# A weight piece of block 2's in-projection becomes filling work in the mixer attention

## The chip, the cores and the metric

One core of one Trainium2 chip. The metric is the device time of one execution in microseconds; 2487.95 us is the median of three runs of the kernel before.

## The reference, cut to what matters

Two transformer blocks of two layers each, at a model width of 1024 and 256 tokens; the change acts on block 2. Each of its layers computes, in the mixer:

```
z = h @ w_in                       # h: normed x, 256 x 1024
m_qk, m_v, m_o, m_i, m_f, c_glu, f_q, f_k, f_v, f_f = split(z)
hm = mlstm(silu(conv(m_qk)), m_v, m_i, m_f)   # 4 heads of 64, normed, times sigmoid(m_o)
hc = silu(layernorm(conv(a * sigmoid(g))))    # a, g = halves of c_glu
hf = softmax(f_q f_k^T / 8 + decay, causal) f_v    # 8 heads of 64
x = x + concat(hm, hc, hf) @ w_out
```

After it come attention over a memory of 256 rows (whose values are `mem_n @ w_kv`) and a feed-forward part. Everything is float32.

## The kernel before, in words

**Products.** All weights come as a stream of pieces of 1 MB, 128 x 2048, through a ring of 6 slots that SyncE fills. ScalarE rounds a piece to fp32r (`ring_hi`, line 235), VectorE takes the rest (`ring_lo`, line 238), and TensorE multiplies three times (high by high, high by low, low by high), all at line 244. A piece serves two groups of products (`pe_products`, line 264); a group is 8 tiles of the contraction by 3 matmuls, 24 matmuls of 256 columns into one bank of PSUM. `take_products` (line 307) is the other side, on ScalarE and VectorE: at the first group of a piece it first splits pieces ahead (`split_ahead`, line 224: two further pieces; at places one more), then waits for the group, copies its bank out, and runs its step for this group. TensorE runs its own step ahead of a group.

**The in-projection of block 2** has 26 groups (`b2_groups`, line 1781), 13 pieces. Groups 22 to 25 are the values of the eight softmax heads, one piece for heads 0 to 3 and one for 4 to 7, written to `tok`. Beside the groups runs the work on what they gave (lines 1812, 1847, 1905), at group numbers written out by hand: at CONV a convolution; at MEANS (17) TensorE's mean for the layer norm; in their step of group 18 VectorE centres (line 1955) and ScalarE loads a table and squares (line 1861, semaphore `head_squared`); at VARS (20) TensorE's matmuls for the variance, which wait for the two squares; in the step VARS ScalarE's root, in the step VARS + 1 VectorE's scaling (line 1967, semaphore `ln_scaled`), in the step VARS + 2 VectorE's split of one piece more; in ScalarE's step UNITS − 1 (22) a table load, six SiLUs (lines 1869, 1872) and the split of one piece more; in its step UNITS + 1 (24) another table load.

**The mixer attention** (`pe_attention`, line 705, and its two partners) goes over 12 pairs of heads and query tiles: 8 of softmax attention, 4 of the mLSTM. It has 15 steps. In step i TensorE makes the scores of pair i, turns (transposes, line 737) the probabilities of pair i − 2 and mixes pair i − 3 with the values. VectorE adds mask and takes the maximum into a score buffer (line 826), and scales by the inverse sum (line 852) one step later; ScalarE takes the exponentials (line 790), copies the turned probabilities (line 798) and the mixed output (line 803). Score buffers are three, of two halves, in `hT`, which lies over the low part of `h`. Output banks are 4 and 5 in turn for the first six pairs, then 4 alone. After TensorE's first scores all three engines meet (line 199): each waits until the others are through with the in-projection.

**Filling.** In steps 9 to 13 TensorE also works off the two groups of one later piece, the memory's values (`pe_value_fill`, line 2113), in bank 5: 16 steps of three matmuls, four amid steps 9, 10 and 11, two after 12 and 13. ScalarE copies them out in its steps 10 and 14 (line 321). In its step 0 ScalarE splits a piece ahead and, in steps 0 and 1, rounds two tiles of the convolution's output (line 516) for the out-projection, in the place where the high part of `h` was; VectorE takes their rests in steps 2 and 3 (line 521). The out-projection goes over its 8 tiles in the order MIXER_TILES, that in which they are split.

Of the kernel before, what the change touches and what calls it, by code (L numbers as in the profile page):

```python
# [107 lines left out]
def build(nc, A, y_out):  # L108
    with ExitStack() as ctx:
# [55 lines left out]
        def sem(name):  # L165
            if name not in sems:
                sems[name] = ctx.enter_context(nc.semaphore(name))
            return sems[name]
# [6 lines left out]
        def base(e, name):  # L175
            return seen.get((e.engine, name), 0)
# [505 lines left out]

        def s_buf(pair, i, e):
            b = 2 * (i % BUF) + e
            if "late" in pair:
                return Zt[:, 8 + b, 0:T]
            return hflat[:, b * 514:(b + 1) * 514] if pair["sinks"] else hT[:, b, 0:T]
# [1076 lines left out]
        def rms2(c):  # L1764
            return Zt[:, 12 + c, T:2 * T]

        MIXER_TILES = (2, 3, 4, 5, 6, 7, 0, 1)
        MIXER_BANKS = (0, 1, 6, 7)


# [10 lines left out]
        def b2_groups(layer):  # L1781
            g = feature_major([z2(8), z2(9)], 0, T)
            g += feature_major([z2(6), z2(7)], 0, T)
            for c in range(2):
                terms, rows_, n, _, held = g[c]
                g[c] = (terms, rows_, n, [("function", z2(8 + c), ACT.Sigmoid)], held)
                terms, rows_, n, _, held = g[2 + c]
                g[2 + c] = (terms, rows_, n, [("gated", CP[:, c, 30:30 + T], z2(8 + c), act_outs[layer] + c + 1)], held)
            g += feature_major([UP[:, 0, 3:259], UP[:, 1, 3:259]], 0, T)
            g += feature_major([UP[:, 2, 3:259], UP[:, 3, 3:259]], 0, T)  # L1790
            g += token_major([SG[:, t, :] for t in range(2)], n=16)
            g += token_major([tok[:, t * 768:t * 768 + 256] for t in range(2)])
            for out, (terms, rows_, n, _, held) in zip((z2(4), z2(5)), feature_major([None, None], 0, T)):
                g.append((terms, rows_, n, [("function", out, ACT.Sigmoid)], held))
            for j in range(2):
                g += feature_major([z2(10 + 2 * j), z2(11 + 2 * j)], 0, T, HD ** -0.5)
            for j in range(2):
                g += feature_major([z2(14 + 2 * j), z2(15 + 2 * j)], 0, T)
            for j in range(2):
                g += token_major([tok[:, t * 768 + 256 + 256 * j:t * 768 + 512 + 256 * j] for t in range(2)])  # L1800
            return g


        B2_WHO = ["act", "act", "dve", "dve"] + 22 * ["act"]
        act_outs = [0, 0]
        B2_BANKS = (2, 3, 0, 1)
        x_outs = [0, 0]

        gated_outs, heads_before = [0, 0], [0, 0]
        GATES, CONV, SUMS, MEANS, VARS, UNITS = 11, 14, 15, 17, 20, 23  # L1810

        def pe_mixer(pe, layer):

# [160 lines left out]
        def causal(q):  # L1974
            return const("masks", 512, 640) if q == 0 else const("masks", 384, 640)

        def fox_pairs():
            pairs = []
            for c in range(4):
                for q in range(TT):  # L1980
                    nk, at = (q + 1) * P, slice(q * P, (q + 1) * P)
                    pairs.append(dict(apart=None, turns=0, alone=c == 3, nk=nk, mask=causal(q), init=[3 * NEG] * 2, sinks=None,
                        scores=[[(Zt[r, 10 + c, at], Zt[r, 14 + c, 0:nk], nk), (row_of(4 + 2 * c + e), falls[:, 0:nk], nk)]
                                for e, r in enumerate(HALVES)],
                        v=[[fv(t, 2 * c + e) for t in range(q + 1)] for e in range(2)],
                        place=[(r, slice(0, P)) for r in HALVES], out=mixT[:, 4 + c, at]))
            return pairs

        def mlstm_pairs():
            pairs = []  # L1990
            for c in range(2):
                for q in range(TT):
                    nk, at = (q + 1) * P, slice(q * P, (q + 1) * P)
                    pairs.append(dict(turns=None, alone=True, nk=nk, mask=causal(q), init=[0.0] * 2, floor=[FC[:, q, 2 * c + e:2 * c + e + 1] for e in range(2)],
                        sinks=None, apart=[(Zt[r, c, at], Zt[r, 2 + c, 0:nk]) for r in HALVES],
                        scores=[[(row_of(2 * c + e), falls[:, 0:nk], nk)] for e in range(2)],
                        v=[[mv(t, 2 * c + e) for t in range(q + 1)] for e in range(2)],
                        place=[(r, slice(0, P)) for r in HALVES], out=Zt[:, 6 + c, at]))
            return pairs


        def act_mix_step(act, layer):

            def step(i):
                act_value_fill(act, i)
                if i < 2:
                    act.wait_ge(sem("conv_ready"), 2 * layer + i + 1)
                    act_split_mix(act, (2 + i,), T)
                c = (i - 5) // 2
                if i % 2 == 1 and 0 <= c < 4:  # L2010
                    act.wait_ge(sem("heads_out"), heads_before[layer] + 2 * c + 2)
                    act_split_mix(act, (4 + c,), T)
                if i == 13:
                    act_m_square(act, layer, 0)
            return step

        def dve_mix_step(dve, layer):

            def step(i):
                if i == 0:  # L2020
                    phase_others(dve)
                if i in (2, 3):
                    dve_split_mix(dve, (i,), T)
                c = (i - 7) // 2
                if i % 2 == 1 and 0 <= c < 4:
                    dve_split_mix(dve, (4 + c,), T)
                dve_value_fill(dve, i)
            return step
# [79 lines left out]


        FILL_BANK = 5  # L2110
        FILL_AMID, FILL_AFTER, FILL_OUT, FILL_PIECE = {9: 4, 10: 4, 11: 4}, {12: 2, 13: 2}, (10, 14), 12

        def pe_value_fill(pe, layer):
            groups, weights = value_groups(1), []
            todo = [(g, k) for g in range(2) for k in range(KT)]
            out = base(pe, "product_out_act")
            meet = meet_first(pe)

            def fill(n):
                for g, k in [todo.pop(0) for _ in range(n)]:  # L2120
                    if (g, k) == (0, 0):
                        pe.wait_ge(sem("heads_out"), heads_before[layer] + 6)
                        weights.extend(piece_slot(pe))
                    if (g, k) == (1, 0):
                        pe.wait_ge(sem("product_out_act"), out + 1)
                    stationary, moving = groups[g][0][k]
                    for m, (w, part) in enumerate(((weights[0], 0), (weights[0], 1), (weights[1], 0))):
                        last = k == KT - 1 and m == 2
                        mm(pe, bank[FILL_BANK][:, 0:T], stationary(w, part), moving(w, part), start=k == 0 and m == 0,
                           stop=last, last_of="product_in_act" if last else None)  # L2130
                    if (g, k) == (1, KT - 1):
                        stream["release"] = True
                        advance(pe, "product_out_act", 2)

            def amid(i):
                fill(FILL_AMID.get(i, 0))

            def between(i):
                meet(i)
                fill(FILL_AFTER.get(i, 0))  # L2140
            return dict(amid=amid, between=between)

        def act_value_fill(act, i):
            if i == 0:
                split_ahead(act, "act", 1)
                wanted["act"] -= 1
            if i == FILL_OUT[0]:
                take_products(act, "act", value_groups(1)[0:1], "act", at=(FILL_BANK,))
            if i == FILL_OUT[1]:
                take_products(act, "act", value_groups(1)[1:2], "act", at=(FILL_BANK,))  # L2150

        def dve_value_fill(dve, i):
            if i == FILL_PIECE:
                take_products(dve, "dve", value_groups(1), "act", at=(FILL_BANK,))

        def x_pairs(layer):
            return [dict(apart=None, turns=1, alone=False, nk=T, mask=const("masks", 128, 384), init=[3 * NEG] * 2, sinks=None,
# [613 lines left out]
        def _(pe):  # L2771
# [25 lines left out]
            for layer in range(DEPTH):  # L2797
# [5 lines left out]
                                inside=lambda k: pe_mean(pe, 4, (3, 4, 5, 6, 7), 0, T) if k == 3 else None)  # L2803
                pe_products(pe, b2_groups(layer), "h_split", B2_WHO, at=B2_BANKS, before=pe_mixer(pe, layer))
                pe.wait_ge(sem("product_out_act"), base(pe, "product_out_act") - 2)
                heads_before[layer] = base(pe, "heads_out")
                pe_attention(pe, fox_pairs() + mlstm_pairs(), **pe_value_fill(pe, layer))
                pe.wait_ge(sem("neg_max"), base(pe, "neg_max"))
# [407 lines left out]
```

## Time and profile before

| | |
|---|---|
| Median of three runs | 2487.95 us (2487.22 to 2489.45) |
| The profiled execution's own time | 2489.04 us |
| Its span, first to last instruction | 2487.3 us |
| Mean granted TensorE clock | 0.992 |
| TensorE matmuls busy | 2398.9 us (96%) |
| TensorE weight loads busy | 2042.9 us (82%) |
| VectorE busy | 1827.4 us (73%) |
| ScalarE busy | 1494.0 us (60%) |

Rows of the profile name a line of the kernel, an engine, an operation and its tiles, out<-in. PE is the TensorE matmul, PEld its weight load, DVE VectorE, ACT ScalarE. A clock of 1.00 is 2.4 GHz, 0.50 is 1.2 GHz. In a row of the timeline, brackets at the end give the engine's idle time before it and what ended it; a matmul's duration contains a tail in which the next one already runs.

### The profile page before, as it was taken

What the parts mean: (1) busy time and instruction counts of PE and PEld (TensorE: products, weight loads), DVE (VectorE), ACT (ScalarE), POOL (GpSimd) and SP (SyncE); (2) the same over time, 40 slices, a digit from 0 to 9 for tenths busy, and PEclk for the clock granted to TensorE, in tenths of its full rate; (3) what the DMA queues carried; (4) which work ended last, traced back from release to release, by engine and by line L of the source; (5) the groups of instructions that cost most, each with busy time, mean ns of one, the idle gap of its engine ahead of it and who ended that gap; (6) DMA issues with size and microseconds to landing.
All of it is one profiled execution on the core that took longest, in us unless ns stands there. A gap on an engine that the chain in (4) does not pass through costs nothing.

```text
span 2487.3 us, 38102 instructions
## 1 busy us (share of the span) xinstructions
PE 2398.9 (96%) x14832; PEld 2042.9 (82%) x14832; DVE 1827.4 (73%) x2487; ACT 1494.0 (60%) x1960; POOL 27.5 (1%) x86
## 2 busy tenths in 40 slices
PE   8997999999999899999999999989999999999998
PEld 6875788888887688898888889788888888888886
DVE  5548766566566777676666657578898898898997
ACT  4246465465444666556665545666777777777775
POOL 0000000000000000010000001000000000000000
PEclk9999999999999999999899999999999999999999
DMA  8245445555544555554235545146998998998996
GB/s 335 105 145 193 156 168 187 186 186 187 186 159 146 221 185 188 186 179 153 86 140 197 189 169 196 69 153 236 372 355 340 371 359 346 361 363 350 359 361 256
DMA packets 81640, 564.57 MB, mean 227 GB/s; under 512 B 9328, under 2 KB 12672, under 8 KB 13632
## 3 DMA queue, kind: packets, MB, share of 16 engines
q1 hardware_dynamic: 80144, 559.97, 60.3%
q0 software_dynamic: 1328, 2.25, 0.3%
q8 instruction: 119, 1.95, 0.3%
q14 instruction: 49, 0.40, 0.1%
HBM read 559.97 MB, written 1.05 MB: 226 GB/s over the span
## 4 chain that ended last, share of the span: by engine, by line
PE 60%; DVE 4%; ACT 3%; issue 1%; DVEq 0%; ACTq 0%
PE psum L244 58%; DVE ring_lo L238 1%; ACT ring_hi L235 1%; PE psum L2428 1%; PE psum L737 1%; ACT Z L798 0%; ACT hT L790 0%; DVE xT L337 0%; DVE hT L398 0%; DVE hT L1489 0%; ACT Z L790 0%; DVE xT L671 0%; DVE Z L1466 0%; DVE Z L1467 0%; DVE xT L669 0%
## 5 line engine op out<-in xcount | busy, mean ns | idle before, releaser
L238 DVE TENSOR_TENSOR ring_lo<-ring,ring_hi 128x2048 fp32r<-128x2048 f32 x477 | 1092.0, 2290 | 272.8 <-ACT ring_hi L235 267.2
L235 ACT ACTIVATE ring_hi<-ring 128x2048 fp32r<-128x2048 f32 x477 | 912.2, 1914 | 332.6 <-PE psum L244 328.3
L244 PE MATMUL psum<-h_parts,ring_hi 128*128 128x512 f32 (+1 forms) x3184 | 861.0, 350 | 10.2 <-DVE h_parts L451 4.1
L244 PE MATMUL psum<-h_parts,ring_lo 128*128 128x256 f32 (+1 forms) x2464 | 601.3, 291 | 0.0
L244 PEld LDWEIGHTS psum<-h_parts,ring_hi 128*128 128x128 f32 x3184 | 515.5, 190 | 37.2 <-issue 12.3
L244 PE MATMUL psum<-ring_hi,h_parts 128*128 128x512 f32 (+1 forms) x1952 | 541.3, 364 | 1.7 <-DVE h_parts L449 0.8
L244 PEld LDWEIGHTS psum<-h_parts,ring_lo 128*128 128x128 f32 x2464 | 466.2, 189 | 72.3
L244 PEld LDWEIGHTS psum<-ring_hi,h_parts 128*128 128x128 f32 x1952 | 344.1, 189 | 53.9 <-DVE h_parts L449 1.2
L244 PE MATMUL psum<-ring_lo,h_parts 128*128 128x512 f32 (+1 forms) x976 | 352.2, 361 | 0.0
L244 PE MATMUL psum<-ring_hi,Zr 128*128 128x512 f32 x704 | 219.3, 393 | 0.0
L244 PEld LDWEIGHTS psum<-ring_lo,h_parts 128*128 128x128 f32 x976 | 184.4, 189 | 28.8
L244 PE MATMUL psum<-Zr,ring_hi 128*128 128x512 f32 x704 | 192.2, 394 | 0.0
L644 DVE TENSOR_TENSOR mixT<-psum,mixT 128x512 f32<-128x512 f32 x88 | 60.9, 692 | 145.1 <-ACT mixT L620 145.0
L244 PEld LDWEIGHTS psum<-ring_hi,Zr 128*128 128x128 f32 x704 | 130.3, 188 | 26.1 <-DVE ring_lo L238 0.2
L244 PE MATMUL psum<-ring_lo,Zr 128*128 128x512 f32 x352 | 137.2, 390 | 0.0
L620 ACT ACTIVATE mixT<-psum 128x512 f32<-128x512 f32 x88 | 52.5, 596 | 139.6 <-PE psum L244 139.5
L244 PEld LDWEIGHTS psum<-Zr,ring_hi 128*128 128x128 f32 x704 | 120.3, 189 | 16.2
L244 PEld LDWEIGHTS psum<-Zr,ring_lo 128*128 128x128 f32 x704 | 108.0, 189 | 15.0
L244 PE MATMUL psum<-Zr,ring_lo 128*128 128x256 f32 x704 | 112.0, 281 | 0.0
L244 PE MATMUL psum<-mix_lo,ring_hi 128*128 128x256 f32 (+1 forms) x336 | 100.1, 298 | 0.0
L244 PE MATMUL psum<-Z 64*128 64x128 f32 (+3 forms) x536 | 67.2, 365 | 20.4 <-DVE Z L1467 8.7
L244 PEld LDWEIGHTS psum<-ring_lo,Zr 128*128 128x128 f32 x352 | 66.1, 188 | 14.2
(297 smaller groups left out, 2111.7 us busy)
## 6 DMA issues: line engine op xcount, KB each, us to landing
ring<-in_stream SPq DMA_DIRECT2D x524, 1024.0 KB, 4.8
Z<-in_first_mods SPq DMA_DIRECT2D x5, 1024.0 KB, 16.8
cst<-in_constants SPq DMA_DIRECT2D x1, 1216.0 KB, 8.1
mixT<-mixT POOLq DMA_DIRECT2D x32, 35.5 KB, 3.9
xT<-in_xT SPq DMA_DIRECT2D x1, 1024.0 KB, 5.7
xT<-in_ctxT SPq DMA_DIRECT2D x1, 1024.0 KB, 8.1
xT<-in_memT POOLq DMA_DIRECT2D x1, 1024.0 KB, 6.0
out_y<-hT SPq DMA_DIRECT2D x4, 256.0 KB, 2.5
```

Of the source, the lines that this page charges most:

```text
L235: e.activation(hi, raw, ACT.Copy).then_inc(sem("piece_rounded"), 1)
L238: e.tensor_tensor(lo, raw, hi.bitcast(F32), ALU.subtract).then_inc(sem("piece_split"), 1)
L244: ins = pe.matmul(*args, **kw)
L620: act.activation(up_rests(f), up_parts(run, f)[1], ACT.Copy).then_inc(sem("up_rest"), 1)
L644: dve.tensor_tensor(up_sums(f), up_parts(run, f)[0], up_rests(f), ALU.add)\
L737: ins = pe.transpose(bank[2 + e][:, b * P:(b + 1) * P], s_buf(p, j, e)[:, b * P:(b + 1) * P], const("ident"))
L2428: ins = pe.transpose(bank[2 + j % 2][:, c * P:(c + 1) * P], hid_tok[j % 2][:, c * P:(c + 1) * P], const("ident"))
```

## The change

The last piece of the in-projection (values of heads 4 to 7) leaves it: 24 groups are left. It becomes filling work ahead of the memory's values, in bank 5: 32 steps of three matmuls, 16 in steps 0 to 5, 16 in steps 7 to 13. Since the filling needs both parts of `h`, the mixer's score buffers go to a tile of `Z`, and the two tiles of the convolution are rounded in ScalarE's steps 6 and 8 and their rests taken in VectorE's steps 8 and 10; MIXER_TILES follows. Bank 5 is taken throughout, so all pairs put their output into bank 4. The piece that ScalarE split in step 0 is split in step 10, and one that it split in the in-projection is split in step 2 (VectorE: step 3). VARS and UNITS come one group earlier. TensorE waits for `ln_scaled` ahead of the attention.

```diff
         def s_buf(pair, i, e):
             b = 2 * (i % BUF) + e
+            if "mixer" in pair:
+                return Zt[:, 18 + b // 2, b % 2 * T:(b % 2 + 1) * T]
...
-        MIXER_TILES = (2, 3, 4, 5, 6, 7, 0, 1)
+        MIXER_TILES = (4, 2, 5, 3, 6, 7, 0, 1)
...
-            for j in range(2):
-                g += token_major([tok[:, t * 768 + 256 + 256 * j:t * 768 + 512 + 256 * j] for t in range(2)])
+            g += token_major([tok[:, t * 768 + 256:t * 768 + 512] for t in range(2)])
...
-        B2_BANKS = (2, 3, 0, 1)
+        B2_BANKS = (0, 1, 2, 3)
...
-        GATES, CONV, SUMS, MEANS, VARS, UNITS = 11, 14, 15, 17, 20, 23
+        GATES, CONV, SUMS, MEANS, VARS, UNITS = 11, 14, 15, 17, 19, 22
...
-                    pairs.append(dict(apart=None, turns=0, alone=c == 3, nk=nk, ...
+                    pairs.append(dict(mixer=True, apart=None, turns=0, alone=True, nk=nk, ...
...
-                if i < 2:
-                    act.wait_ge(sem("conv_ready"), 2 * layer + i + 1)
-                    act_split_mix(act, (2 + i,), T)
+                if i in (6, 8):
+                    act.wait_ge(sem("conv_ready"), 2 * layer + (i - 6) // 2 + 1)
+                    act_split_mix(act, (2 + (i - 6) // 2,), T)
...
-                if i in (2, 3):
-                    dve_split_mix(dve, (i,), T)
+                if i in (8, 10):
+                    dve_split_mix(dve, (2 + (i - 8) // 2,), T)
...
-        FILL_AMID, FILL_AFTER, FILL_OUT, FILL_PIECE = {9: 4, 10: 4, 11: 4}, {12: 2, 13: 2}, (10, 14), 12
+        FILL_AMID, FILL_AFTER = {7: 2, 8: 2, 9: 2, 10: 2, 11: 4}, {0: 3, 1: 3, 2: 2, 3: 3, 4: 3, 5: 2, 12: 2, 13: 2}
+        FILL_OUT = {2: 0, 5: 1, 10: 2, 14: 3}
+        FILL_PIECE = {3: 0, 12: 2}
+
+        def fill_groups():
+
+            late = token_major([tok[:, t * 768 + 512:t * 768 + 768] for t in range(2)])
+            return late + value_groups(1)
...
             def fill(n):
                 for g, k in [todo.pop(0) for _ in range(n)]:
-                    if (g, k) == (0, 0):
-                        pe.wait_ge(sem("heads_out"), heads_before[layer] + 6)
-                        weights.extend(piece_slot(pe))
-                    if (g, k) == (1, 0):
-                        pe.wait_ge(sem("product_out_act"), out + 1)
+                    if k == 0 and g % 2 == 0:
+                        weights[:] = piece_slot(pe)
+                    if k == 0 and g > 0:
+                        pe.wait_ge(sem("product_out_act"), out + g)
...
         def act_value_fill(act, i):
-            if i == 0:
-                split_ahead(act, "act", 1)
-                wanted["act"] -= 1
-            if i == FILL_OUT[0]:
-                take_products(act, "act", value_groups(1)[0:1], "act", at=(FILL_BANK,))
-            if i == FILL_OUT[1]:
-                take_products(act, "act", value_groups(1)[1:2], "act", at=(FILL_BANK,))
+            if i in FILL_OUT:
+                g = FILL_OUT[i]
+                take_products(act, "act", fill_groups()[g:g + 1], "act", at=(FILL_BANK,))
 
         def dve_value_fill(dve, i):
-            if i == FILL_PIECE:
-                take_products(dve, "dve", value_groups(1), "act", at=(FILL_BANK,))
+            if i in FILL_PIECE:
+                g = FILL_PIECE[i]
+                take_products(dve, "dve", fill_groups()[g:g + 2], "act", at=(FILL_BANK,))
...
                 pe.wait_ge(sem("product_out_act"), base(pe, "product_out_act") - 2)
+                pe.wait_ge(sem("ln_scaled"), 2 * layer + 1)
```

## Rows read from the trace of the kernel before

**Rows 1.** The page: the span, TensorE's busy time, the chain's shares by engine

```profile
span 2487.3 us, 38102 instructions
...
PE 2398.9 (96%) x14832; PEld 2042.9 (82%) x14832; DVE 1827.4 (73%) x2487; ACT 1494.0 (60%) x1960; POOL 27.5 (1%) x86
...
PE 60%; DVE 4%; ACT 3%; issue 1%; DVEq 0%; ACTq 0%
```

**Rows 2.** Stretches of both attentions (stretch, length, busy time of each engine, clock, DMA)

```profile
1168.30:1174.60 6.30, 4.43 (x28) 2.70 (x26) 3.35 (x21) 5.01 (x15) 0.00 (x0) 0.96 0.49 169
1174.60:1195.00 20.40, 19.61 (x97) 13.55 (x98) 11.42 (x64) 11.91 (x53) 0.00 (x0) 0.51 0.00 0
1195.00:1208.50 13.50, 13.06 (x108) 9.59 (x106) 10.52 (x44) 7.88 (x29) 0.00 (x0) 1.00 0.01 2
1566.60:1573.90 7.30, 4.64 (x29) 2.85 (x28) 4.29 (x25) 5.75 (x18) 0.00 (x0) 0.97 0.38 144
1573.90:1580.80 6.90, 6.90 (x36) 4.54 (x38) 3.44 (x19) 3.17 (x14) 0.00 (x0) 0.53 0.00 0
1580.80:1604.20 23.40, 20.75 (x169) 14.95 (x169) 17.46 (x86) 15.66 (x61) 0.00 (x0) 1.00 0.01 1
```

**Rows 3.** TensorE's waits: first row layer 0's attention, the others layer 1's

```profile
PE psum L737 <- ACT Z L798: 1.9, 2, 1.7
...
PE psum L737 <- ACT Z L798: 3.5, 4, 1.7
PE psum L737 <- DVE hT L852: 0.7, 1, 0.7
PE psum L244 <- ACT mixT L803: 0.5, 1, 0.5
```

**Rows 4.** TensorE's timeline, layer 0: variance, group 20, group 22, last matmul of group 25

```profile
1150.05 1.10 PE L244 MATMUL psum<-Z,cst 128*128 128x256 f32 x4
1150.80 0.59 PE L244 MATMUL psum<-h_parts,ring_hi 128*128 128x256 f32 x2
...
1156.74 0.41 PE L244 MATMUL psum<-ring_hi,h_parts 128*128 128x256 f32 x2
...
1168.14 0.28 PE L244 MATMUL psum<-ring_lo,h_parts 128*128 128x256 f32 x1
```

**Rows 5.** ScalarE's timeline, layer 0: the squares; the long step of group 22 and after

```profile
1149.48 0.75 ACT L1861 ACTIVATE Z<-Z 128x256 f32<-128x256 f32 x2 [0.45 <-DVE Z L1955]
...
1160.22 1.28 ACT L1869 ACT_TABLE_LOAD   x1
1161.52 1.34 ACT L1869 ACTIVATE Z<-Z 128x256 f32<-128x256 f32 x4
1162.76 0.89 ACT L1872 ACTIVATE mixT<-Z,vec 128x256 f32<-128x256 f32 x2
1163.56 1.90 ACT L235 ACTIVATE ring_hi<-ring 128x2048 fp32r<-128x2048 f32 x1
1165.37 0.63 ACT L321 ACTIVATE tok<-psum 128x256 f32<-128x256 f32 x2
1166.01 1.28 ACT L1877 ACT_TABLE_LOAD   x1
```

**Rows 6.** VectorE's timeline, layer 0: a split, centring, scaling, the last split

```profile
1146.69 2.29 DVE L238 TENSOR_TENSOR ring_lo<-ring,ring_hi 128x2048 fp32r<-128x2048 f32 x1 [4.33 <-ACT ring_hi L235]
...
1149.04 0.75 DVE L1955 SCALAR_TENSOR_TENSOR Z<-psum,Z 128x256 f32<-128x256 f32 x2
...
1155.28 0.88 DVE L1967 SCALAR_TENSOR_TENSOR Z<-Z,vec 128x256 f32<-128x256 f32 x2 [0.23 <-ACT Z L1865]
...
1165.50 2.29 DVE L238 TENSOR_TENSOR ring_lo<-ring,ring_hi 128x2048 fp32r<-128x2048 f32 x1 [4.04 <-ACT ring_hi L235]
```

**Rows 7.** TensorE's timeline, layer 0: filling matmuls at the low clock

```profile
1193.09 0.65 PE L244 MATMUL psum<-ring_hi,h_parts 128*128 128x256 f32 x2
1193.54 0.41 PE L244 MATMUL psum<-ring_lo,h_parts 128*128 128x256 f32 x1
```

More of the change, by code:

```diff
@@ L1981, in fox_pairs @@
                     nk, at = (q + 1) * P, slice(q * P, (q + 1) * P)
-                    pairs.append(dict(apart=None, turns=0, alone=c == 3, nk=nk, mask=causal(q), init=[3 * NEG] * 2, sinks=None,
+                    pairs.append(dict(mixer=True, apart=None, turns=0, alone=True, nk=nk, mask=causal(q), init=[3 * NEG] * 2, sinks=None,
                         scores=[[(Zt[r, 10 + c, at], Zt[r, 14 + c, 0:nk], nk), (row_of(4 + 2 * c + e), falls[:, 0:nk], nk)]
@@ L1993, in mlstm_pairs @@
                     nk, at = (q + 1) * P, slice(q * P, (q + 1) * P)
-                    pairs.append(dict(turns=None, alone=True, nk=nk, mask=causal(q), init=[0.0] * 2, floor=[FC[:, q, 2 * c + e:2 * c + e + 1] for e in range(2)],
+                    pairs.append(dict(mixer=True, turns=None, alone=True, nk=nk, mask=causal(q), init=[0.0] * 2, floor=[FC[:, q, 2 * c + e:2 * c + e + 1] for e in range(2)],
                         sinks=None, apart=[(Zt[r, c, at], Zt[r, 2 + c, 0:nk]) for r in HALVES],
@@ L2110, in build @@
         FILL_BANK = 5
-        FILL_AMID, FILL_AFTER, FILL_OUT, FILL_PIECE = {9: 4, 10: 4, 11: 4}, {12: 2, 13: 2}, (10, 14), 12
+        FILL_AMID, FILL_AFTER = {7: 2, 8: 2, 9: 2, 10: 2, 11: 4}, {0: 3, 1: 3, 2: 2, 3: 3, 4: 3, 5: 2, 12: 2, 13: 2}
[4 more added lines that the diff above has]
+            return late + value_groups(1)
         def pe_value_fill(pe, layer):
-            groups, weights = value_groups(1), []
-            todo = [(g, k) for g in range(2) for k in range(KT)]
+            groups, weights = fill_groups(), []
+            todo = [(g, k) for g in range(4) for k in range(KT)]
             out = base(pe, "product_out_act")
@@ L2130, in fill @@
                            stop=last, last_of="product_in_act" if last else None)
-                    if (g, k) == (1, KT - 1):
+                    if k == KT - 1 and g % 2 == 1:
                         stream["release"] = True
```

## The prediction

> **What bounds the kernel now.** The page first: TensorE is busy 96% of 2487.3 us, and 60% of the chain that ended last is its own time [rows 1]. So I read only what TensorE does where the change acts: the tail of block 2's in-projection and the mixer attention behind it, once per layer, some 110 us in all. The table by stretch [rows 2] cuts the attention, from the last in-projection matmul to the first out-projection one, where the granted clock changes. Layer 0 takes 1168.3 to 1208.5 (40.2 us), of which 20.4 us at clock 0.51 (that is 1.2 GHz), with TensorE busy 19.61 us. Layer 1 takes 1566.6 to 1604.2 (37.6 us), of which only 6.9 us at the low clock. The waits [rows 3] show what TensorE's pauses wait for: 1.9 us in layer 0 and 3.5 us in layer 1 for ScalarE's copies of the turned probabilities, 0.7 for the first probabilities, 0.5 for a head's output. The reader is to see that the pauses are short, and that the first (1.7 us, inside those 1.9 and 3.5) stands just before the clock falls, in both layers.
>
> In the table the pauses are 6.30+20.40+13.50 less 4.43+19.61+13.06 = 3.1 us in layer 0, and 37.6 less 4.64+6.90+20.75 = 5.3 us in layer 1.
>
> **1. The piece leaves the in-projection.** Two groups of 24 matmuls. From 1156.74 to 1168.26 there are four such groups [rows 4], so 0.12 us a matmul and 2.88 us a group: −5.76 us per layer.
>
> **2. VARS moves from 20 to 19.** TensorE does the layer norm's variance matmuls ahead of group VARS. They need ScalarE's two squares, in its step of group 18. That step isn't moved. ScalarE squares at 1149.48, each about 0.37 us [rows 5], and can't sooner: VectorE centres at 1149.04, behind the 2.29 us split of a weight piece that it starts at 1146.69 [rows 6]. Today TensorE comes to these matmuls at 1150.05 [rows 4], 0.2 us after the first square is there, so nothing shows. One group earlier it comes at 1150.05 − 2.88 = 1147.17 and waits until about 1149.9: **+2.7 us** per layer, a new wait on the path, with groups 19 to 23 queued behind it and nothing else to cover it. Layer 1 repeats the pattern to 0.1 us.
>
> **3. The meeting of the engines at the attention's start.** ScalarE's long step (table load, four and two SiLUs, the split of a piece, two copies, another table load) now hangs on group 21 and has two groups behind it, not three. From its rows 1160.22, 1161.52, 1162.76, 1163.56, 1165.37 and 1166.01 [rows 5]: 1.3+1.24+0.80+1.81+0.64+1.28, with the copy of group 21 (0.4) and latency 7.6 us after that group's end. VectorE's half of the split, 2.29 us [rows 6], starts when ScalarE's is done and ends at about 8.0. TensorE is there after 2 × 2.88 plus the first pair's scores (0.96) = 6.7. It pauses 1.2 to 1.4 us, for VectorE last, where it paused 0.3. Before, a third group of 2.88 us covered this. The new wait for ln_scaled costs nothing: VectorE scales at 1155.3 today [rows 6] and at about 1160 then, 5 us ahead of TensorE.
>
> **4. The filling.** 32 steps of three matmuls, where there were 16. The pairs' own work first: busy less the 16 old steps (5.76) is 37.1 − 5.8 − 0.5 (for the steps that ran at the low clock: two matmuls take 0.45 there [rows 7], 0.24 at 2.4 GHz) = 30.8 us in layer 0, and 32.3 − 5.8 = 26.5 in layer 1. They differ by 4.3 us for 11.9 us more at the low clock (19.6 less 0.8 of pauses' edges and filling, against 6.9). So a microsecond at the low clock costs 0.36 us of the pairs' work, and at full clock it is 26.5 − 0.36 × 6.9 = **24.0 us**. Filling: 32 × 0.36 = **11.5 us**. Pauses after the change:
> - the meeting, 1.3;
> - the first filled group's eviction: ScalarE's step 2 now splits a piece (1.9 us) ahead of that copy, and TensorE needs the bank in step 3: 1.0, with the mixing and the scores of pair 4 behind it;
> - the same in step 10: a split of 1.9 us, then the copy; TensorE wants the bank in step 11, behind it the scores of pair 11: 2.2. The split stood in step 0 before;
> - steps 9 and 10 filled four steps each between decays and scores, now two; the wait for scores_read that these covered comes out, 0.8 twice;
> - left of the old 0.8 us waits for ScalarE's copies, 0.2.
>
> These pauses are estimates, got by carrying the three engines' rows forward step by step; each may be 0 or a half larger. Sum 6.3, less overlap taken as 6.0. The attention is then 24.0+11.5+6.0 = **41.5 us** in either layer, if the clock stays up: +1.3 against layer 0's 40.2, +3.9 against layer 1's 37.6. VectorE's split of 2.29 us in step 3 delays pair 4's scores by less than the filling that TensorE still has. The old first pause, 1.7 us, goes: ScalarE's split of step 0 and its two tiles no longer stand before the first copies.
>
> **5. One output bank.** TensorE's mixing of pair j waits for the copy of pair j−1's output. That copy (0.27 us) ends over 1 us before, behind scores and turning: nothing. The last pairs do so already. Score buffers in another tile: same shapes, nothing. The order of the out-projection's tiles follows the order of their splitting: nothing. Its last two tiles come as late behind the attention as before.
>
> **The clock.** In both layers it fell after a stretch with about half its time idle at the second and third pair. With filling there it should not. By the trace alone, 13.5 and 23.4 us at 1.00 with TensorE 97% and 89% busy [rows 2] show that fill and pairs together hold it. The pause of 2.7 us at VARS, though, is longer than those. It may cost nothing, or the clock for 6.9 us, the shorter stretch of [rows 2], in which dense matmuls at 0.22 us for 0.12 [rows 4, 7] lose 3 us. I take the middle, once in the two layers: **+1.4 us**, with both ends kept, in each layer, for the range.
>
> The Trainium skill, "TensorE: Matmul & The Clock Gate", Part 4 (PE-mode transpose), says that transposes don't count as busy the way other matmuls do. Here layer 0 ran 20.4 us at the low clock while 96% busy, which agrees; layer 1 rose without any filling, which a strict reading doesn't give. By the rule the filling would be what holds the clock, and the sum is the one above.
>
> **The sum.** Layer 0: −5.76+2.7+1.3 = −1.8. Layer 1: −5.76+2.7+3.9 = +0.8. Clock +1.4. Together +0.4 us. The profiled execution took 2489.04 us; the median of the three runs is 2487.95, 1.1 below. I put the sum on the median: **2488.5 us**.
>
> **Rivals.**
> - *VARS doesn't stall, or the attention hides more.* Then each layer gains 2.7 us more: 2488.5 − 5.4 − 1.4 (no clock fall) = 2481.7; with step 11's wait gone too, 2477. For it: only that TensorE's place at VARS is worked out. Against it: rows 5 and 6 leave no earlier square. Some gain can also come from pauses that I set too long. Chance 0.2.
> - *The clock stays low (slower).* It falls at the pause at VARS or the one at the meeting, in both layers, and the attention's small matmuls don't raise it, as from 1174.6 to 1195.0 today. With the filling, TensorE would be the bound throughout: 20.4 us at the low clock cost 0.36 to 0.45 × 20.4 = 7.3 to 9 us over 41.5. Both layers: 2488.5 + 16 = 2504. It decides from about 6 us at the low clock per layer on (6 × 0.4 × 2 = 4.8 us). Against it: filling matmuls came with the rise at 1194.6. Chance 0.13, shorter stretches among it (2493 to 2496).
> - The Trainium skill, same page, "A second HAM failure mode: psum-queue depth-cycling", says that micro-pauses between groups, with banks cycled, make the clock go up and down. That is the mechanism of this rival with its price taken from rows; in layer 1 pauses of 0.8 us at full clock didn't do it.
> - *Nothing moves*: what leaves the in-projection comes back whole in the attention. That is the forecast, 0.67.
>
> **The numbers.** About 0.2% (5 us) is what a measurement of this kernel can tell from no change. Faster than 2483: 0.20. Within: 0.67. Slower than 2493: 0.13. The range is 2481 to 2494: the first rival's end below, a few stretches of low clock above.
>
> **What would show it.** A TensorE pause of 2.7 us for ScalarE's squares (line 1861) ahead of the variance matmuls; the in-projection shorter by 3 us, not 5.8; a pause of over 1 us at the meeting; waits for the copy into tok of 1 and 2 us; clock 1.00 through the attention in both layers, which then take 41 to 42 us each. Wrong, if that first pause isn't there, if the attention stays under 38 us, or if a clock of 0.50 stands for over 10 us.

## The result, and the profile after

The changed kernel takes **2502.0 us** (median of 5 runs, 2499.8 to 2503.5) where the kernel before takes 2487.95: ratio 1.0052, 95% interval 1.0041 to 1.0063. It is slower by 14 us. The forecast was 2488.5, no change, with a range of 2481 to 2494. Its profiled execution took 2501.9 us, of a span of 2500.1.

TensorE's waits over layer 0's part of the change, from the squares to the out-projection; layer 1 has the first four rows again, to 0.1 us (columns: who waited for whom, us in total, times, longest):

```profile
PE psum L244 <- ACT tok L321: 3.1, 2, 2.0
PE psum L244 <- ACT Z L1862: 2.7, 1, 2.7
PE psum L244 <- DVEq L190: 1.6, 1, 1.6
PE psum L244 <- DVE sc L844: 1.4, 2, 0.7
PE psum L739 <- ACT Z L800: 0.2, 1, 0.2
```

Every pause of the prediction's list is here: 2.7 us for the squares, 1.6 at the meeting (1.2 to 1.4 were forecast), 1.05 and 2.0 for the copies into tok (1.0 and 2.2), 0.7 twice (0.8 twice), 0.2. Of [rows 3] the first is left, with 0.2 us (line 739 is line 737 of the kernel before). What the list lacks is in the clock. The timeline of TensorE, VectorE and ScalarE at VARS, layer 0:

```profile
1152.64 2.05 PE L244 MATMUL psum<-Z,cst 128*128 128x256 f32 x4 [2.74 <-ACT Z L1862]
1154.13 0.99 PE L244 MATMUL psum<-h_parts,ring_hi 128*128 128x256 f32 x2
...
1149.29 2.29 DVE L238 TENSOR_TENSOR ring_lo<-ring,ring_hi 128x2048 fp32r<-128x2048 f32 x1 [4.33 <-ACT ring_hi L235]
...
1151.64 0.75 DVE L1956 SCALAR_TENSOR_TENSOR Z<-psum,Z 128x256 f32<-128x256 f32 x2
...
1152.09 0.75 ACT L1862 ACTIVATE Z<-Z 128x256 f32<-128x256 f32 x2 [0.45 <-DVE Z L1956]
```

The chain of split, centring and squares is that of [rows 5, 6]. The four variance matmuls take 2.05 us, where [rows 4] has 1.10: they run at 1.2 GHz. The clock fell at 1152.2, still in the pause, for 3.4 us. In layer 1 they take 1.10, and the clock falls 1.2 us after their start, in group 19, again for 3.4 us, in which two matmuls take 0.63 us, for 0.40 ahead of the pause:

```profile
1553.78 1.10 PE L244 MATMUL psum<-Z,cst 128*128 128x256 f32 x4 [2.73 <-ACT Z L1862]
1554.53 0.61 PE L244 MATMUL psum<-h_parts,ring_hi 128*128 128x256 f32 x2
1554.96 0.40 PE L244 MATMUL psum<-h_parts,ring_lo 128*128 128x256 f32 x1
1555.16 0.63 PE L244 MATMUL psum<-h_parts,ring_hi 128*128 128x256 f32 x2
1555.59 0.41 PE L244 MATMUL psum<-h_parts,ring_lo 128*128 128x256 f32 x1
```

The stretches of the kernel after (stretch, length, busy time of each engine, clock, DMA): the fall at VARS; layer 0's meeting with the pause, the fall behind it, the rest of layer 0's attention; layer 1's attention and the fall at its end:

```profile
1152.60:1156.10 3.50, 3.46 (x14) 3.13 (x15) 0.94 (x3) 0.23 (x1) 0.00 (x0) 0.57 0.00 0
1169.50:1173.10 3.60, 2.00 (x15) 1.77 (x15) 2.96 (x6) 2.09 (x5) 0.00 (x0) 0.94 0.54 159
1173.10:1176.60 3.50, 3.50 (x18) 2.62 (x16) 1.11 (x7) 0.72 (x5) 0.00 (x0) 0.57 0.32 136
1176.60:1212.50 35.90, 31.13 (x249) 22.92 (x247) 25.96 (x117) 25.50 (x91) 0.00 (x0) 1.00 0.09 31
1570.70:1606.60 35.90, 29.75 (x229) 22.54 (x230) 25.62 (x118) 25.32 (x87) 0.00 (x0) 0.99 0.17 60
1606.60:1613.50 6.90, 6.90 (x37) 4.47 (x35) 4.42 (x11) 2.56 (x9) 0.00 (x0) 0.54 0.00 1
```

Read from TensorE's timeline, first matmul of the norm's mean (MEANS) to first score, and first score to first out-projection matmul:

```
                    in-projection's tail      attention
                    layer 0    layer 1        layer 0   layer 1
before              27.8       27.8           40.2      37.5
after               26.3       26.4           43.1      44.3
after, second trace 26.4       26.4           44.3      41.6
```

So the tail gave 1.4 to 1.5 us, not 3.0 (27.82 − 5.76 + 2.74 = 24.80; the other 1.5 to 1.6 us are matmuls at the low clock at VARS), and the attention took 3 to 7 us more, where +1.3 and +3.9 were forecast.

### The profile page after: what moved, and what is told of

It is laid out like the page before. It is cut to its first block, busy times and chain, and to the rows that moved or that the text cites. A ratio compares the mean times of both kernels' runs of the same rounds, so it can differ in the third digit from the quotient of the medians.

```text
span 2500.1 us, 38106 instructions
## 1 busy us (share of the span) xinstructions
PE 2403.3 (96%) x14832; PEld 2047.8 (82%) x14832; DVE 1828.2 (73%) x2487; ACT 1493.3 (60%) x1960; POOL 27.6 (1%) x86
## 3 DMA queue, kind: packets, MB, share of 16 engines
HBM read 559.97 MB, written 1.05 MB: 224 GB/s over the span
## 4 chain that ended last, share of the span: by engine, by line
PE 59%; DVE 4%; ACT 3%; issue 1%; DVEq 0%; ACTq 0%
PE psum L244 57%; DVE ring_lo L238 2%; ACT ring_hi L235 1%; PE psum L2432 1%; PE psum L739 0%; ACT Z L792 0%; ACT Z L800 0%; DVE hT L398 0%; DVE xT L337 0%; DVE hT L1491 0%; DVE Z L828 0%; DVE xT L671 0%; DVE Z L1468 0%; DVE Z L1469 0%; DVE xT L669 0%
## 5 line engine op out<-in xcount | busy, mean ns | idle before, releaser
L244 PE MATMUL psum<-h_parts,ring_hi 128*128 128x512 f32 (+1 forms) x3184 | 864.1, 351 | 10.2 <-DVE h_parts L451 4.1
L244 PEld LDWEIGHTS psum<-ring_lo,Zr 128*128 128x128 f32 x352 | 66.1, 188 | 14.1
```

The source lines that it names most:

```text
L244: ins = pe.matmul(*args, **kw)
```

## The experiments

All times are medians; a ratio is against the kernel before, run beside it (2489.1 to 2489.6 us in these jobs), with its 95% interval. To place the difference I cut each trace at four ScalarE instructions that all kernels have: the convolution's output and the root of the m norm, of either layer. The stretch between the two of one layer holds all that the change touches there. In brackets, the time at the low clock:

```
                      ahead          layer 0       between        layer 1       behind
before                1133.2 ( 3.4)  80.0 (20.5)   318.3 ( 0.0)   77.4 ( 6.8)   878.4 ( 9.2)
before, second trace  1133.3 ( 3.4)  78.9 (13.7)   319.8 ( 3.4)   77.3 (10.2)   878.4 ( 9.0)
after                 1135.8 (13.7)  81.4 ( 6.8)   319.7 ( 3.4)   82.7 (10.2)   880.5 (16.7)
after, second trace   1133.8 ( 3.4)  82.8 (10.2)   319.8 ( 3.4)   80.0 ( 3.4)   879.3 (12.6)
before_vars19         1134.0 (10.2)  81.6 (13.7)   319.8 ( 3.4)   84.2 (23.9)   878.7 ( 9.9)
dummies               1131.8 ( 0.0)  81.6 (13.7)   319.8 ( 3.4)   80.1 (10.2)   879.7 (13.2)
vars20                1135.1 (10.2)  79.4 (10.2)   319.7 ( 3.4)   78.5 ( 6.8)   879.1 ( 7.6)
unread                1131.6 ( 0.0)  75.8 ( 0.0)   319.8 ( 3.4)   75.8 ( 0.0)   880.2 (13.9)
copy_first            1133.4 ( 6.8)  73.5 ( 0.0)   318.3 ( 0.0)   73.5 ( 0.0)   878.4 ( 9.0)
copy_first_19         1131.9 ( 3.4)  79.3 ( 6.8)   318.4 ( 0.0)   77.8 ( 3.4)   878.7 (10.0)
split_later           1133.4 ( 3.4)  75.6 ( 3.4)   319.8 ( 3.4)   74.8 ( 0.0)   880.1 (15.9)
fill_then_meet        1132.1 ( 3.4)  72.3 ( 0.0)   318.4 ( 0.0)   72.3 ( 0.0)   880.3 (16.3)
```

The code ahead, between and behind is untouched in all of them, and yet moves by up to 4, 1.5 and 2 us, mostly with the time at the low clock (between: 318.3 or 318.4 us without a fall, 319.7 to 319.8 with one of 3.4 us): where the clock falls there is another place from one execution to the next. In the last column 4 to 7 us of the low clock stand behind TensorE's last matmul and cost nothing. One trace can't price a change of this size by its span; the stretches of the two layers and the medians can.

Every execution has its own mean granted clock on record, not only the traced ones. The time at the low clock that it gives is (1 − clock) × 2 × span, within 2.5 us by rounding; here its mean over all executions of a kernel, beside the median time:

```
                      executions   median us   low clock, mean us
before, beside them   71           2489.2      39.9
after                 5            2502.0      49.0
after, second set     4            2497.9      38.7
before_vars19         5            2501.2      62.0
dummies               11           2495.0      45.8
vars20                12           2488.2      29.0
unread                11           2485.7      22.1
copy_first            5            2479.7      17.9
copy_first_19         11           2490.0      25.8
```

**same_before and same_after** are the two kernels unedited, with second traces.

> The kernel before, unedited, once more with a trace. Theory T (the change costs what its own stretches show, and the 6 us found in code that the change doesn't touch are chance of where the clock's falls come): the time is 2488 within 2 us, but the clock falls at other places, and the code ahead of block 2 moves by 1 to 3 us against the first trace. Rival R (the program as a whole is placed or loaded differently, and the untouched code is slower for good): this trace has the same time up to block 2 as the first one, within 0.5 us.

> The kernel after, unedited, once more with a trace. T: 2502 within 2 us; the pauses are the same to 0.1 us (2.7 for the squares, 1.6 at the meeting, 1.05 and 2.0 for the copies into tok, 0.7 twice), the clock's falls are at other places. R: the first mixer begins again 2.4 us later than in the kernel before.

2489.4 us (ratio 1.0000, 0.9991 to 1.0009) and 2497.9 us (1.0039, 1.0024 to 1.0053; 4 runs). Neither theory fits as it was put. T missed the time of the kernel after: 2497.9 for 2502 within 2 us. Its intervals in the two sets overlap, and the loss is 9 to 14 us. The kernel before doesn't move up to block 2 (1133.3 for 1133.2), which R asked; but the kernel after begins block 2's mixer 0.6 us later in its second trace, not 2.4, which falls against R and for T. One of R's claims fell, and one of T's (that the first kernel's own code ahead moves by 1 to 3 us) was only seen in later kernels. The pauses of the kernel after repeat to 0.1 us.

**vars20 and before_vars19** take the step VARS by itself, from both sides. The diff is that of vars20, on the kernel after; before_vars19, on the kernel before, turns 20 into 19, leaves UNITS at 23, and writes 22 for VARS + 2.

```diff
-        GATES, CONV, SUMS, MEANS, VARS, UNITS = 11, 14, 15, 17, 19, 22
+        GATES, CONV, SUMS, MEANS, VARS, UNITS = 11, 14, 15, 17, 20, 22
...
-                if g == VARS + 2:
+                if g == 21:
                     split_ahead(dve, "dve", 1)
```

> The kernel after with VARS back at 20 (VectorE's split of one piece more stays in step 21). T: the 2.7 us pause for the squares goes in both layers, and the clock's fall behind it with it: 5.4 us and 1.4 us for each fall, so 2502 - 8.2 = 2494, between 2492 and 2496.5. Rival M (the meeting hides it: what comes before it is waited for anyway, because the long step of ScalarE hangs on group 21): ScalarE's step moves along with group 21, so M would hold only if something else ended last there; then 2500 to 2502.

> The kernel before with nothing but VARS at 19 (VectorE's extra split stays in step 22). T: a pause of 2.7 us per layer and a fall of the clock behind it in most layers: 2488 + 5.4 + 2.8 = 2496, between 2493 and 2498. Rival H (the pause is hidden where the long step has three groups behind it, and only the change as a whole uncovers it): 2488 to 2490.

vars20: 2488.2 us (0.9998, 0.9989 to 1.0006; 12 runs from 2483.8 to 2494.1). before_vars19: 2501.2 us (1.0046, 1.0033 to 1.0059). Both moved the way of T and further than it allowed. VARS at 19 alone makes the kernel before 12 us slower, which is about the changed kernel's whole loss (14.1 and 8.8 us in its two sets); and without it the change neither gains nor loses. The pause is 2.7 us in both layers of before_vars19 and gone in vars20. M and H are out. In before_vars19 the clock fell at VARS in both layers, again in the attention for longer (13.7 and 23.9 us low in all), as its row above shows; the timeline of layer 0's variance matmuls:

```profile
1150.94 2.05 PE L244 MATMUL psum<-Z,cst 128*128 128x256 f32 x4 [2.73 <-ACT Z L1861]
```

**dummies** is before_vars19 with 20 matmuls in the pause: it keeps the pause as time and takes the idleness out of it. The matmuls' results go to a bank that is free then, and nothing reads them.

```diff
                 if g == VARS:
+                    for _ in range(20):
+                        mm(pe, bank[5][:, 0:T], h(0, 0, 0, P), h(0, 0, 0, T), start=True, stop=True)
                     for c in range(2):
                         await_next(pe, "head_squared")
```

> The kernel before with VARS at 19 (2501.2) and, in the pause of 2.7 us ahead of the variance matmuls, 20 matmuls of 0.12 us that nobody reads, so that TensorE waits only 0.3 us. It splits the loss into pause and clock. Theory C (the pause is 2.7 us, and what comes on top is the clock that falls behind it, four times out of four so far, with the variance matmuls at half speed): the clock no longer falls there, 1.8 us a layer come back and more where the fall shifted later ones: 2493 to 2496. Rival P (the excess over 5.4 us has another cause than the clock): 2499 to 2501.

2494.95 us (1.0027, 1.0017 to 1.0036; 11 runs), as theory C had it. TensorE's timeline of dummies, the 20 matmuls and the variance matmuls behind them:

```profile
1145.75 2.56 PE L244 MATMUL psum<-h_parts 128*128 128x256 f32 x20
1148.55 1.13 PE L244 MATMUL psum<-Z,cst 128*128 128x256 f32 x4 [0.24 <-ACT Z L1863]
```

1.13 us for 2.05, in layer 0. The kernel is now 5.7 us slower than before, and 2 x 2.7 = 5.4 are the pause. The other 6.3 us of before_vars19 (2501.2 − 2494.95) are the clock: over all executions dummies has 16 us less at the low clock, so 0.39 us of time for each. That is more than the two falls of 3.4 us at VARS; others went with them. In the one trace of each, layer 1's stretch shows this (80.1 us for 84.2, with 10.2 us low for 23.9), layer 0's doesn't (81.6 in both, with 13.7 us low in both).

**one_bank** takes the parts that the prediction costed at nothing: the kernel before with the mixer's score buffers at Zt[:, 18 + b // 2, ...] and alone=True in all pairs.

> The kernel before with the mixer's score buffers in the tile of Z and all outputs in bank 4; nothing else is changed. Theory (free, as the prediction has it): 2488.5 to 2490, the same as before. Rival (each mixing now waits for the copy of the output before, and 6 pairs a layer lose 0.2 us or more): 2491 to 2494.

2489.4 us (0.9998, 0.9989 to 1.0007; 11 runs). Free, and its layers' stretches are those of the kernel before to 0.2 us.

**copy_first** is vars20 with ScalarE's order changed in its steps 2 and 10; **copy_first_19** the same with VARS at 19.

```diff
-                take_products(act, "act", fill_groups()[g:g + 1], "act", at=(FILL_BANK,))
+                take_products(act, "act", fill_groups()[g:g + 1], "act", at=(FILL_BANK,), held_back=(0,))
+                if g in (0, 2):
+                    split_ahead(act, "act")
```

> The kernel after with VARS at 20 (2488.2) and, in ScalarE's steps 2 and 10, the filled group's copy ahead of the split of a piece, not behind it. Theory W (TensorE's waits of 1.05 and 2.02 us for tok are that split's 1.9 us, and are on the path): they shrink to 0.2 or less, 2.7 us per layer come back, and the clock stays up in the steps behind: 2481 to 2484. Rival Q (the exponentials and copies of the next step, which now stand behind the split, make TensorE wait for these instead): 2486 to 2489.

> The kernel after with the copies ahead of the splits and VARS left at 19. Against copy_first (2479.7) it has the pause at VARS: 2.7 us and a fall of the clock of 1.8 us, each layer: 2479.7 + 9 = 2488.7, between 2487 and 2491. Rival (the two edits aren't additive, the fall at VARS brings later ones with it): 2492 or more.

copy_first: 2479.7 us (0.9965, 0.9951 to 0.9979), 1.3 below theory W's range. copy_first_19: 2490.0 us (1.0000, 0.9991 to 1.0009), 10.3 more, the price of VARS again and inside what was expected; its layers' stretches are 5.8 and 4.3 us longer than copy_first's. Here is what copy_first removes, in the kernel after: ScalarE's timeline in step 10, the copy behind the split, and what TensorE's first matmul of the next group waited for:

```profile
1202.64 1.90 ACT L235 ACTIVATE ring_hi<-ring 128x2048 fp32r<-128x2048 f32 x1
1204.44 0.38 ACT L321 ACTIVATE tok<-psum 128x256 f32<-128x256 f32 x1
...
1204.87 0.39 PE L244 MATMUL psum<-ring_hi,h_parts 128*128 128x256 f32 x1 [2.02 <-ACT tok L321]
```

And the waits of copy_first, layer 0's attention:

```profile
PE psum L244 <- DVEq L190: 1.6, 1, 1.6
PE psum L244 <- DVE sc L844: 1.4, 2, 0.7
PE psum L739 <- ACT Z L800: 0.7, 2, 0.5
PE psum L244 <- ACT tok L321: 0.2, 1, 0.2
```

Against vars20, whose waits there are 3.1 us for the copies into tok, 1.6 and 1.4, waits are 2.2 us fewer per layer (3.1 against 0.2 + 0.7), but the layers' stretches are 5.9 and 5.0 us shorter. Their attentions, first vars20, then copy_first:

```profile
1164.50:1209.90 45.40, 39.26 (x278) 29.32 (x277) 30.05 (x129) 28.43 (x98) 0.00 (x0) 0.89 0.14 47
1563.70:1608.10 44.40, 38.14 (x278) 28.15 (x277) 30.02 (x129) 28.39 (x98) 0.00 (x0) 0.92 0.13 48
```

```profile
1162.90:1202.20 39.30, 35.26 (x277) 26.27 (x276) 29.93 (x129) 28.17 (x98) 0.00 (x0) 1.00 0.15 55
1554.70:1594.00 39.30, 35.26 (x277) 26.27 (x276) 29.90 (x129) 28.14 (x98) 0.00 (x0) 1.00 0.15 55
```

The same matmuls keep TensorE busy for 4.0 and 2.9 us less: in vars20 some ran at 1.2 GHz. In copy_first the clock is 1.00 throughout, although the meeting's pause of 1.6 us is still there in both layers.

**unread** tells shorter waits and the clock apart: vars20 with the pauses kept as time and filled with unread matmuls in free banks, 12 ahead of the meeting, 8 in step 3, 16 in step 11.

```diff
+                    if k == 0 and g == 1:
+                        pe.wait_ge(sem("scores_read"), base(pe, "scores_read") + 6)
+                        unread(8, 0)
+                    if k == 0 and g == 3:
+                        pe.wait_ge(sem("heads_out"), heads_before[layer] + 8)
+                        unread(16, 4)
...
+                if i == 0:
+                    unread(12, 4)
                 meet(i)
```

> vars20 (2488.2) with matmuls that nobody reads in its three long pauses: 12 ahead of the meeting, 8 ahead of the wait for the first copy into tok, 16 ahead of that in step 11, 0.12 us each. Nothing waits for less: the pauses stay as time, only TensorE is busy in them. Theory C (half of what copy_first won was not the 2.4 us of pauses per layer but the clock that no longer fell): the clock stays at 1.00 through both attentions, and the time is 2481 to 2484.5. Rival P (it was all waiting): 2487 to 2489.

2485.7 us (0.9985, 0.9976 to 0.9994; 11 runs). It lies between the two, above what theory C gave and below the rival, and its interval overlaps that of vars20. The traces are clearer than the medians. The attentions of unread:

```profile
1161.10:1202.80 41.70, 39.76 (x314) 30.66 (x313) 30.05 (x129) 28.31 (x98) 0.00 (x0) 1.00 0.15 52
1556.70:1598.40 41.70, 39.75 (x314) 30.65 (x313) 30.04 (x129) 28.31 (x98) 0.00 (x0) 1.00 0.15 51
```

Both at 1.00, and 3.7 and 2.7 us shorter than vars20's, with the same pauses kept as time. vars20's trace is one of its slower executions (2493.6 us for a median of 2488.2), so on average the clock in the attention costs less than these 6.4 us: 2.6 by the medians, with 6.9 us less at the low clock over all executions.

**Which pauses the clock fell at.** All pauses of TensorE of 1 us and more in the two layers' stretches, from the traces of all kernels here; a fall counts if it starts in the pause or at most 1.6 us behind it:

```
pause                                                              falls
2.7 us, at VARS (after twice, before_vars19, copy_first_19)        8 of 8
2.0 us, step 11 (after twice, vars20)                              4 of 6
1.6 us, meeting (after twice, vars20, copy_first, copy_first_19)   3 of 10
1.8 us, turned probabilities (split_later)                         1 of 2
1.7 us, the same (before twice, one_bank, before_vars19, dummies)  7 of 7
1.0 us, meeting (split_later)                                      0 of 2
1.05 us, step 3 (after twice, vars20)                              0 of 6
```

At VARS the falls start from 0.5 us before the pause's end to 1.3 us behind it. The length of a pause alone doesn't settle it: in the old schedule (fifth line) the clock fell in three more attentions, of same_before, before_vars19 and dummies, without any pause over 0.9 us. In unread, fill_then_meet and fill_then_meet_late, which have no pause of 1 us, it fell in none of six.

**split_later** moves the last split from ahead of the meeting into the attention: no extra split in step UNITS − 1 and in VectorE's step 21, group 22's held back, and

```diff
         def act_value_fill(act, i):
+            if i == 0:
+                split_ahead(act, "act")
...
         def dve_value_fill(dve, i):
+            if i == 1:
+                split_ahead(dve, "dve")
```

> As copy_first, and the piece of the memory's values is split in step 0 (ScalarE) and step 1 (VectorE) of the attention, not ahead of it, so that VectorE's 2.3 us no longer stand before the meeting. Theory M (the pause of 1.6 us at the meeting is VectorE's split): it falls to about 0.5, 1.1 us per layer: 2 us below copy_first. Rival V (VectorE's split in step 1 stands before the scaling of pair 1 and the maxima of pair 2 instead): TensorE pauses there, and the time is that of copy_first or up to 3 us above.

2486.7 us (0.9989, 0.9980 to 0.9998; 11 runs), 7 above copy_first, further than rival V went. Its waits, layer 0's attention:

```profile
PE psum L739 <- ACT Z L800: 2.1, 2, 1.8
PE psum L244 <- DVE sc L844: 1.4, 2, 0.7
PE psum L244 <- ACTq L190: 1.0, 1, 1.0
PE psum L244 <- ACT tok L321: 0.2, 1, 0.2
```

The pause at the meeting fell from 1.6 to 1.0, where M said 0.5 (that split was what TensorE waited for last; now it is ScalarE's sign), and a pause of 1.8 us for the turned probabilities' copies came up in its place. 3.4 us of the 7 are in the layers' stretches; in these two traces the rest isn't in code that differs.

**fill_then_meet** is copy_first with step 0's filling ahead of the meeting; **fill_then_meet_late** has one filling step each amid 7 and 8 and three amid 9 and 10.

```diff
             def between(i):
+                if i == 0:
+                    fill(FILL_AFTER[0])
                 meet(i)
-                fill(FILL_AFTER.get(i, 0))
+                if i:
+                    fill(FILL_AFTER.get(i, 0))
```

> copy_first (2479.7) with step 0's three filling steps (1.08 us) ahead of the meeting, not behind it. Theory (TensorE sits 1.6 us at the meeting for VectorE's split and can work meanwhile): the pause falls to 0.5 and 1.1 us per layer come off: 2477.5. Rival (ScalarE and VectorE wait for TensorE's own sign at the meeting, which now comes 1.1 us later, and the second pair is late by as much): 2479 to 2481.

> As fill_then_meet, and of the memory's values one step each amid 7 and 8 and three each amid 9 and 10 (two everywhere before), where TensorE waits 0.7 us for scores_read. Theory: the two waits of 0.7 shrink to 0.35 and steps 7 and 8 are shorter by 0.36 each: 0.7 us per layer, 2476. Rival (the first group's end in step 10 comes no sooner, so nothing moves): the same as fill_then_meet.

**2477.5 us** (0.9955, 0.9941 to 0.9968) and 2478.4 (0.9952, 0.9939 to 0.9966). The first is as forecast: the pause at the meeting is 0.5 us, and either layer's stretch is 1.2 us shorter than copy_first's. The second can't be told from it by time. Its stretches are 71.9 for 72.3, 0.4 less per layer, where 0.7 was expected. These beat both the kernel before and the changed one.

## Why the prediction was wrong

**1, the piece leaves: right.** In vars20 the tail from MEANS to the first score is 22.06 us in both layers, for 27.82: 5.76 less, as forecast.

**2, VARS: right in the mechanism, half in the price.** The pause was forecast at +2.7 and is 2.7, in four of four layer executions of the kernel after. The step that failed is the last sentence of the part on the clock, "I take the middle, once in the two layers: +1.4". The clock fell at that pause in all four, and in both layers of before_vars19 and copy_first_19. One such pause costs 2.7 us and about 1.6 us of slow matmuls right at it: 4.3 us per layer, 8.6 for both, where the prediction had 6.8 with its +1.4. In medians VARS costs more still, 12.1 us on the kernel before and 10.3 on copy_first; dummies splits the 12.1 into 5.7 for the pause and 6.3 to 6.4 for the clock.

**3, the meeting: right in kind**, 1.6 us where 1.2 to 1.4 were forecast, and VectorE's split is what it waits for (split_later).

**4, the filling: right at full clock.** The prediction gave the attention 41.5 us "if the clock stays up". unread, which holds it up and waits as long, measures 41.7 in both layers. The list of pauses was good to 0.3 us each, the 24.0 + 11.5 + 6.0 to 0.2. What failed is the sentence "With filling there it should not", of the clock's fall. The old fall, at the second and third pair, is gone as forecast; falls came behind the new pauses instead, the meeting's 1.6 us and step 11's 2.0, at other places in each trace (1173 and 1606 us in one, 1203 us in the other of the kernel after), so that its attentions take 41.6 to 44.3 us. The price per microsecond at the low clock, 0.36, was about right: vars20's 10.2 and 6.8 us low against unread cost 3.6 and 2.7, 0.35 and 0.40. I had priced a fall well and counted too few. The sign of being wrong that I had set, a clock of 0.50 for over 10 us, doesn't come up in the kernel after: its longest fall there is 6.8 us. It asked for one long fall, and the loss came in several short ones.

**5, one output bank, buffers: right**, nothing (one_bank).

**The sum** in medians: vars20 − 0.9 against the kernel beside it, where the forecast without the VARS stall was about −6 (the first rival, 2481.7); of the 5.5 us between them unread gives back 2.6 to 3.1 by holding the clock in the attention; the rest isn't placed, for in the traces unread's two stretches are 4.5 to 5.8 us shorter than those of before, near the forecast. Then VARS, +10 to +14. The forecast's +2.7 x 2 + 1.4 for it made 6.8. The table of the low clock closes this sum within its noise: from vars20 to the two sets of the kernel after there are 20 and 10 us more at the low clock, and 13.8 and 9.7 us of time; less 5.4 of pause that is 0.42 and 0.44 us for each of them.

**The rivals.** The first, no stall at VARS or an attention that hides more, didn't come: the stall was there in every layer. The slower rival ("the clock stays low") was the right kind, but not in the form that was priced: no 20 us at the low clock in the attention, but several short falls at new pauses, and it deserved far more than 0.13. The Trainium skill, "TensorE: Matmul & The Clock Gate", "A second HAM failure mode: psum-queue depth-cycling", describes something like it, of another kernel: frequent short idle times between groups of matmuls, with banks cycled, make the clock go down and up, and that is paid for between them. The traces here agree that it goes down at idle times and up again: two falls of 3.4 us stand in the 25 us ahead of the 35.9 us row of layer 0 above, each at a pause. They don't show that it takes many: one pause of 2.7 us was enough, 8 times of 8. Against this rival the prediction had set the pauses of 0.8 us, and those of 0.7 in fill_then_meet indeed brought no fall; it had not asked what those of 1.6 to 2.7 us do. What the Trainium skill, same page, Part 4 (PE-mode transpose), says of transposes wasn't put to a test of its own.

**Open.** The two traces of the kernel after are 10.4 us longer than those of before on average, and some 3.7 of these lie in code that isn't changed. They show more time at the low clock there, but traces of other kernels show as much, and over all executions the kernel after has 49.0 us low in one set and 38.7 in the other, for 39.9 before. So I can't say whether the change moves these falls or whether they are chance. It is also open why taking the idleness out of VARS took away more time at the low clock (16 us) than the two falls there, and what decides whether a pause of 1.6 or 2.0 us brings a fall.

## What to carry to other kernels

When a change puts a new idle pause into TensorE's schedule, price its length and a fall of the clock at it. In these traces that fall came at 3 of 10 pauses of 1.6 us, 4 of 6 of 2.0 and 8 of 8 of 2.7, and a microsecond at the low clock cost about 0.4. The test is cheap: fill the pause with matmuls that nobody reads, and see whether time comes back though the pause stays as long. When a schedule written by step numbers is shortened by one step, look at each number for what it waits on, not only for its order: VARS had 0.2 us of slack, and one group was 2.9. Where an engine both frees a bank that TensorE waits for and prepares something needed much later, do the short copy first: 2.2 us of waits less in each of two layers moved the kernel by 8.5.

## What I hadn't expected of the hardware

A pause of 2.7 us cost more than double its length, 12.1 us for two: in eight of eight layer executions the clock fell at it, and with TensorE kept busy by unread matmuls it didn't fall there and 6.3 us came back. Matmuls of no use made a kernel faster by 0.25%. And identical kernels differ by where their falls lie: the kernel before, in two traces, had 20.5 and 13.7 us at the low clock in layer 0's stretch for 80.0 and 78.9 us.
